# RWKV time mix: bonus sums ahead of the last value projection, beta keys chunk by chunk, a weight split inside the first chunk's preparation

## The reference

```python
def rwkv7_time_mix(h, ...):
    r, k, v = jnp.einsum('sbtc,scd->sbtd', h[None] + dx[None] * mu[:3, None, None, :], w_rkv)
    ...
    a = jax.nn.sigmoid(a0 + (xa @ a1) @ a2)
    kk = (k * k_k).reshape(B, T, H, N)
    kk = kk * lax.rsqrt(jnp.maximum(jnp.sum(kk * kk, axis=-1, keepdims=True), 1e-24))
    k = k * (1 + (a - 1) * k_a)
    # S_t = S_{t-1} diag(decay_t) + (S_{t-1} (-kk_t)) (kk_t a_t)^T + v_t k_t^T ;  y_t = S_t r_t
    y = wkv7_scan(heads(r), heads(decay), heads(k), heads(v), -kk, kk * a_h)
    ...
    bonus = jnp.sum(heads(r) * heads(k) * r_k, axis=-1, keepdims=True)
    y = y + (bonus * heads(v)).reshape(B, T, C)
    return (y * g) @ w_o
```

## Time and profile before

| | |
|---|---|
| median of 3 runs | 2223.61 us (2222.28 to 2227.85) |
| the profiled execution, its own time | 2214.61 us |
| its span, first to last instruction | 2212.9 us |
| TensorE busy | 1926.4 us (87%) |
| VectorE busy | 1326.8 us (60%) |
| ScalarE busy | 823.6 us (37%) |
| GpSimd busy | 630.5 us (28%) |
| granted TensorE clock, mean | 0.976 of full speed |

### The profile page before, as it was taken

The page is one execution under the profiler, slowest core; times in us unless marked ns, Lnnn a source line. Parts: engine busy times, 40 slices in busy tenths (PEclk is TensorE's granted clock), DMA queues, the critical chain, the costliest instruction groups (busy, mean ns, idle before and its releaser), DMA issues.

```text
span 2212.9 us, 30589 instructions
## 1 busy us (share of the span) xinstructions
PE 1926.4 (87%) x11823; PEld 1408.7 (64%) x11823; DVE 1326.8 (60%) x2174; ACT 823.6 (37%) x1281; POOL 630.5 (28%) x620
## 2 busy tenths in 40 slices
PE   6999967876766766668999999899999999989999
PEld 4997843422222222225888888888888888768887
DVE  4777685666656666645544857465456545675554
ACT  2335422221122111212444564354435444474443
POOL 1000177677777777775000001112000000001000
PEclk9999989999999999999999999999999999989999
DMA  9982399999999999995755320036554555424553
GB/s 352 332 274 80 126 354 374 373 375 358 372 363 366 356 365 368 367 380 217 232 190 188 115 96 22 4 115 197 186 190 149 166 187 183 154 76 130 189 189 114
DMA packets 255567, 510.36 MB, mean 231 GB/s; under 512 B 14810, under 2 KB 173228, under 8 KB 252380
## 3 DMA queue, kind: packets, MB, share of 16 engines
q0 software_dynamic: 74416, 270.83, 32.5%
q1 hardware_dynamic: 177898, 233.95, 32.3%
q10 hardware_dynamic: 3138, 4.00, 0.6%
HBM read 507.68 MB, written 1.05 MB: 230 GB/s over the span
## 4 chain that ended last, share of the span: by engine, by line
PE 54%; POOL 21%; issue 8%; DVE 7%; DMA 5%; ACT 3%; another core or an unknown queue 1%; SPq 0%; DVEq 0%; ACTq 0%; POOLq 0%
PE bank L639 22%; POOL big L1687 21%; PE bank L667 11%; PE bank L409 10%; DMA big<-in_peer_v,aux 3%; DMA big<-in_w_mod 2%; PE bank L2355 1%; PE bank L1595 1%; PE bank L369 1%; DVE w_lo L319 1%; PE bank L682 1%; ACT w_hi L315 1%; DVE big L1778 1%; DVE aux L1043 0%
## 5 line engine op out<-in xcount | busy, mean ns | idle before, releaser
L1595 PE MATMUL bank<-big 128*128 128x512 f32 x1008 | 508.2, 629 | 202.3 <-DMA big<-in_peer_v,aux 180.2
L319 DVE TENSOR_TENSOR w_lo<-w_raw,w_hi 128x2048 fp32r<-128x2048 f32 x198 | 453.6, 2293 | 273.3 <-ACT w_hi L315 272.4
L1595 PEld LDWEIGHTS bank<-big 128*128 128x128 f32 x1008 | 175.9, 193 | 513.3 <-DMA big<-in_peer_v,aux 350.4
L1778 DVE SCALAR_TENSOR_TENSOR big<-big,aux 128x1024 f32<-128x1024 f32 x256 | 313.6, 1225 | 260.6 <-DMA big<-in_peer_u,aux 225.8
L315 ACT ACTIVATE w_hi<-w_raw 128x2048 fp32r<-128x2048 f32 x198 | 378.3, 1911 | 230.4 <-PE bank L639 109.7
L1687 POOL DMA_INDIRECT big<-in_peer_v,aux x256 | 288.2, 1126 | 116.4 <-issue 69.8
L1687 POOL DMA_INDIRECT big<-in_peer_u,aux x256 | 268.7, 1050 | 105.6 <-issue 76.7
L1672 ACT ACTIVATE big<-ident,aux 128x128 f32<-128x128 f32 x252 | 99.5, 399 | 501.2 <-PE bank L1595 260.0
L639 PE MATMUL bank<-w_hi,hh 128*128 128x512 f32 x704 | 278.7, 396 | 2.8 <-DVE x L1466 1.7
L639 PE MATMUL bank<-w_lo,hh 128*128 128x512 f32 x704 | 274.2, 389 | 0.0
L639 PE MATMUL bank<-w_hi,hl 128*128 128x512 f32 x704 | 265.5, 390 | 0.0
(11 more groups left out here) (433 smaller groups left out, 2709.9 us busy)
## 6 DMA issues: line engine op xcount, KB each, us to landing
w_raw<-in_ffn_w_in SPq DMA_DIRECT2D x176, 512.0 KB, 4.6
w_raw<-in_ffn_w_out SPq DMA_DIRECT2D x44, 1024.0 KB, 4.9
big<-in_w_mod SPq DMA_DIRECT2D x24, 1024.0 KB, 8.2
w_raw<-in_w_in SPq DMA_DIRECT2D x22, 1024.0 KB, 9.5
w_raw<-in_rwkv_w_rkv SPq DMA_DIRECT2D x12, 1024.0 KB, 5.2
w_raw<-in_peer_w_query SPq DMA_DIRECT2D x8, 1024.0 KB, 5.5
w_raw<-in_w_kv SPq DMA_DIRECT2D x8, 1024.0 KB, 5.6
w_raw<-in_w_out SPq DMA_DIRECT2D x4, 1024.0 KB, 5.2
```

What stands on the lines that cost most here:

```text
L319: dve.tensor_tensor(w_lo[i][:, :], w_raw[i][:, :], w_hi[i][:, :].bitcast(F32), ALU.subtract)\
L1595: mm = pe.matmul(bank[4 + 2 * tt + half][:, :], diag[:, turn % RROWS, :], ring_rows[turn % RROWS][:, half * 512:(half + 1) * 512], start=( ...
L1778: dve.scalar_tensor_tensor(out=row, in0=row, scalar=1.0, in1=h2tok[:, r // P, :], op0=ALU.mult, op1=ALU.mult, accum_out=dots[:, r:r + 1]). ...
```

## The change

Four edits. (1) TensorE makes the bonus sums after projection RKV+10 and before RKV+11, where they stood behind the turned values. (2) The product `aT * kkT` goes into a tile of its own, `removed` (the place of `rT`, free once the queries are made), behind the queries; the beta keys are made from it chunk by chunk, chunk 0 ahead of the recurrence, chunks 1 and 2 behind P of chunk 0, chunk 3 behind T2 of chunk 0. (3) D of chunk c waits for its own beta keys. (4) The split of RKV+13 moves from ahead of bonus_v to behind T3 of chunk 0, and ScalarE waits for it before it writes `x` of chunk 0. The passes themselves are the same in number of elements.

```diff
+        def bonus_sums_pe(pe):
+            pe.wait_ge(S("bonus_rk"), 1)
+            pe.wait_ge(S("head_normed"), 4)
+            for kp in range(4):
+                for k in (2 * kp, 2 * kp + 1):
+                    for g in range(2):
+                        ch = slice(g * DH, (g + 1) * DH)
+                        mm = pe.matmul(bank[4 + kp][ch, (k % 2) * T:(k % 2 + 1) * T], ones[ch, 0:DH], scratch[ch, k, :],
+                                       start=True, stop=True)
+                mm.then_inc(S("bonus_sum"), 1)
...
                 if j == 1:
                     head_spread_pe(pe, 0)
+                if j == 2:
+                    bonus_sums_pe(pe)
...
-            pe.wait_ge(S("bonus_rk"), 1)
-            pe.wait_ge(S("head_normed"), 4)
-            for kp in range(4):
...
-                mm.then_inc(S("bonus_sum"), 1)
             pe.wait_ge(S("wkv_in"), 4)
             pe.wait_ge(S("v_tok"), CHUNKS)
             wkv_pe(pe)
...
                 elif name == "D":
                     if c == 0 and g == 1:
                         pe.wait_ge(S("bonus_v"), 4)
+                    pe.wait_ge(S("wkv_in"), 4 + c)
...
                 if name == "x":
+                    if c == 0:
+                        act.wait_ge(S("w_lo"), RKV + 14)
...
+        removed = fm(bigs(3))
+
+        def beta_keys(dve, c):
+            dve.tensor_tensor(keys[:, :, c, 0], by_chunk(removed)[:, :, c], by_chunk(growth)[:, :, c], ALU.mult)\
+               .then_inc(S("wkv_in"), 1)
...
                 v.then_inc(S("wkv_dve"), 1)
+                if c == 0 and g == 1:
+                    if name == "P":
+                        beta_keys(dve, 1)
+                        beta_keys(dve, 2)
+                    elif name == "T2":
+                        beta_keys(dve, 3)
+                    elif name == "T3":
+                        lo.upto(RKV + 13)
...
             dve.wait_ge(S("head_normed"), 4)
-            o(dve.tensor_tensor(aT, aT, kkT, ALU.mult))
             dve.wait_ge(S("decays"), 2)
...
+            dve.wait_ge(S("wkv_in"), 1)
+            o(dve.tensor_tensor(removed, aT, kkT, ALU.mult))
             dve.wait_ge(S("decays"), 1)
             o.wait()
             dve.wait_ge(S("wkv_in"), 2)
-            dve.tensor_tensor(keys[:, :, :, 0], by_chunk(aT), by_chunk(growth), ALU.mult).then_inc(S("wkv_in"), 1)
-            dve.wait_ge(S("wkv_in"), 3)
             dve.tensor_tensor(keys[:, :, :, 1], by_chunk(keyT), by_chunk(growth), ALU.mult).then_inc(S("wkv_in"), 1)
-            lo.upto(RKV + 13)
+            beta_keys(dve, 0)
             dve.wait_ge(S("v_turned"), CHUNKS)
             for kp in range(4):
                 dve.wait_ge(S("bonus_sum"), kp + 1)
```

More of the change, by code:

```diff
@@ L2411, in y_square_sum, with wkv_dve @@
             return dve.tensor_reduce(y_columns(y_stat, c), y_chunk(bigs(2), c), AXX, ALU.add)
-        def wkv_dve(dve):
+        removed = fm(bigs(3))
+        def beta_keys(dve, c):
+            dve.tensor_tensor(keys[:, :, c, 0], by_chunk(removed)[:, :, c], by_chunk(growth)[:, :, c], ALU.mult)\
+               .then_inc(S("wkv_in"), 1)
+        def wkv_dve(dve, lo):
             def heads(m):
@@ L2678, in rwkv_dve @@
                 dve.tensor_tensor(part, part, bank[4 + kp][:, :], ALU.mult).then_inc(S("bonus_v"), 1)
-            wkv_dve(dve)
+            wkv_dve(dve, lo)
             for c in range(CHUNKS - 1):
```

## The result

| | before | changed |
|---|---|---|
| median (range), 22 runs each | 2223.48 us (2216.49 to 2230.16) | 2229.43 us (2221.05 to 2236.93) |
| ratio, 95% interval | | 1.0025 (1.0013 to 1.0037) |
| the profiled execution's span | 2212.9 us | 2224.9 us |

By the ratio the changed kernel is 5.6 us slower, with an interval of 2.9 to 8.2 us on 2223.5. The 5.6 us lie within the 0.3% (6.7 us) that the prediction called no change; the upper part of the interval does not. The prediction forecast 2.9 us, at the interval's lower edge.

The account below looks back on a forecast made before the run. The prediction took VectorE and TensorE to reach the entry within a microsecond of each other, so relieving VectorE gains nothing. 1.08 (entry) + 0.2 (GpSimd) + 1.61 (split) = 2.9 us, giving 2226.5 us, range 2219 to 2233.

Parts of the forecast that it names:

- TensorE ahead of the entry, the new wait: Before bonus_v: TensorE's gapless 12.91 us is only reordered, so VectorE's 3.9 us gain becomes waiting for the turning.
- Entry, 1.08 us: Start of the recurrence: bonus_v, then DE and P of chunk 0, come 1.08 us later, behind the turning.
- Beta keys of chunks 1 and 2: Behind P of chunk 0: their 1.2 us fit in VectorE's 2.59 us wait for TD and cost VectorE nothing.
- GpSimd, 0.2 us: At the sums for T: beta keys on VectorE slow GpSimd, making TD 0.2 us later, bounds 0 and 0.4.
- The split, 1.61 us: Between T3 of chunk 0 and DE of chunk 1: the moved split of RKV+13 adds 1.61 us to the chain.
- Behind it nothing gives back: From chunk 1 on: nothing in the rest of the recurrence or after it recovers the 2.9 us.
- Rival B, the clock: Thin TensorE stretches at the entry and before DE of chunk 1: clock falls, 2.3 us each; one 0.08, both 0.06.
- Rival A: At the entry: VectorE alone bounds it, bonus_v starts 3.9 us earlier, sum -2.3 us; chance 0.07.
- C: At DE of chunk 1: TensorE ends last and hides the split, so 1.61 goes and 1.3 us is left; chance 0.07.

Follow-up runs that it names:

- bonus_twice: The changed kernel with all bonus sums made twice over in their new place; ratio to the kernel before 1.0018 (1.0002 to 1.0034).
- warm_entry: The changed kernel with six unread matmuls ahead of D of chunk 0, filling TensorE's wait; ratio to the kernel before 1.0013 (0.9998 to 1.0027).
- split_4x: The changed kernel with three more passes like the split of RKV+13 ahead of it; ratio to the kernel before 1.0048 (1.0032 to 1.0063).
- bonus_ahead: The kernel before with only the bonus sums moved between projections RKV+10 and RKV+11; ratio to the kernel before 1.0019 (1.0003 to 1.0034).
- split_back: The changed kernel with the split of RKV+13 back ahead of bonus_v; ratio to the kernel before 1.0011 (1.0000 to 1.0023).
- beta_alone: The kernel before with only the beta keys made chunk by chunk, bonus sums and split in old places; ratio to before 1.0006 (0.9990 to 1.0022).

## Why the prediction was right, and where its terms were off

The verdict held: the time moved the way that was forecast and by less than 0.3%. What bounds the entry and DE of chunk 1 was right and was shown. The size was low, 2.9 us for a measured 5.6, since the entry was under-sized and the clock's fall stood outside the sum; with the 0.3% as the line, this much error did not change the verdict. By its own steps:

- *TensorE ahead of the entry, the new wait*: right. No gap between the pieces, VectorE idle 5.58 us (4.9 forecast), released by the turning.
- *Entry, 1.08 us*: right in mechanism, too small. It was 1.70 in the changed kernel's first profile, and between 1.43 and 1.84 in all profiles with edit 1 alone or whole. In the first, bonus sums, projection and turning took 3.60 + 5.94 + 3.90 = 13.44 us where 13.15 had been reckoned from the earlier trace rows, and RKV+10 ahead of them ended 0.3 late. The half clock from the head norms lasted 6.8 us in both kernels, but began and ended 0.3 us later against the scaling in the changed one.
- *Beta keys of chunks 1 and 2*: hidden, as said. *GpSimd, 0.2 us*: the contention is real, the price nothing. In the second profile of the changed kernel its four sums took 3.77 us in place of 3.08 and ended at 1322.27, 0.18 us ahead of TD, which started on time. The rule of the Trainium skill ("GPSIMD Engine Reference", Key points) held for the two instructions: two beta keys in a row took 1.82 and 2.15 us in the two profiles, not 1.2. The 0.4 us that the prediction drew from it did not come, since the slack ahead of TD was 0.87 us.
- *The split, 1.61 us*: exact. The distance between the two places grew by 1.60 or 1.61 in every profile at full clock that had it.
- *Behind it nothing gives back*: not settled. From the start of DE of chunk 1 to the end of the last y the changed kernel took 78.7 and 77.7 us in its two profiles, before 77.8 and 76.5. At the last y it is thus 5.2 us late in the first pair of profiles and 4.7 in the second. Between the two profiles of one kernel the difference is that of the pauses of 0.2 to 1.3 us on TensorE that the trace calls "issue" (in sum about 6.4 and 4.9 us before, 6.7 and 5.3 in the changed kernel). They make up only 0.3 to 0.4 us of the 0.9 and 1.2 by which the changed kernel took longer; the rest was not traced. On the other side, bonus_twice was 7.8 us late at chunk 1 and only 4.0 slower in time.
- *Rival B, the clock*: this is the term that was most mis-judged. It had one fall at 0.08 with 2.3 us, as a case beside the likeliest. It came in five of six profiles and cost 0.9 to 1.4 us each time. The cause that B named, the thin stretch at the entry, is what the profiles speak for: no fall came without edit 1, or with the wait filled. It is no more than a condition that makes a fall likely, since the second profile of the changed kernel had the same stretch and no fall. The second stretch, ahead of DE of chunk 1, brought no fall in the changed kernel's two profiles; it did in warm_entry (0.84 us) and in split_4x, where the wait is 6.9 us longer and the half clock lasted 10.2 us. The price was over-sized because B took over the 6.30 us of the earlier trace rows for the length of a fall: those at the entry lasted 3.4 us, in which the lower level can cost at most 1.7.
- *Rival A and C*: both refuted, A by bonus_ahead and bonus_twice, C by split_back and split_4x.

With these sizes the sum is 1.7 + 0 + 1.0 + 1.6 = 4.3 us, 3.3 without the fall, against a measured 5.6 (2.9 to 8.2). The interval takes both in. Another 0.9 us is seen between chunk 1 and the last y in the first pair of profiles; whether the change costs it or it is scatter stays open, since no run was fine enough to tell it.

No version tried was faster than before by more than a measurement can tell. The best by its places is beta_alone, 0.86 us ahead at chunk 1. A kernel that writes bonus_v to another place, so that it need not wait for the turning, wasn't tried.

## What to carry to other kernels

When the chain names one engine for a whole stretch, read the engine beside it before taking work off the first: here TensorE worked without a gap for 12.9 us and would have set the entry itself less than a microsecond earlier, so 3.9 us of relief on VectorE became idle time. A pass is free only where its engine waits: moving the split of 2.3 us from a place that has become idle to one with 0.5 us of slack cost 1.6 us. And an edit that leaves TensorE a thinner stretch than before can cost the clock on top, as it did in five of six profiles here.

## What the runs showed of the hardware that was not expected

- The clock: behind stretches with 2.1 us busy of 4 at the entry the granted clock fell to its lower level for 3.4 us in five profiles; in the second profile of the changed kernel it didn't, and with part of the wait filled by unread matmuls it never did at that place in three. "TensorE: Matmul & The Clock Gate" of the Trainium skill, Part 1, has the lower clock as the resting state that activity releases. That filling the wait went with a full clock agrees with it; the stretches of 1.98 and 2.10 us that kept the full clock show that a thin stretch does not always bring a fall.
- A float32 matmul of this stage stands as two records in the trace: keep_warm's six gave 12 of 0.236 us. The texts above count records (the 32 bonus sums are 16 matmuls in the code, the 128 of the turning 64), and the expectation of 1.35 us for six was half of their price.
- With VectorE reading two SBUF inputs beside it, four GpSimd sums took 0.69 us more (3.77 in place of 3.08).
